# Norms between the blocks of a transformer stack, taken by halves of the tokens

## What is computed

```python
def rms_norm(x, g):
    y = x * lax.rsqrt(jnp.mean(x * x, axis=-1, keepdims=True) + NORM_EPS)
    return y * g

h = rms_norm(x, pre)                      # norm before the block
m = mixer(h)                              # or silu(h @ w_gate) * (h @ w_up) @ w_down
x = x + rms_norm(m, post)                 # norm behind the block, added to the stream
```

## Time and profile before

| what | us |
|---|---|
| median of three runs | 1984.16 (1982.49 to 1985.83) |
| the profiled execution | 1984.12 |
| its span, first to last instruction | 1982.3 |
| PE busy | 1939.0 (98% of the span) |
| DVE busy | 837.3 (42%) |
| ACT busy | 415.3 (21%) |
| POOL busy | 1199.4 (61%) |

### The profile page before, as it was taken

One profiled execution on the slowest core, in us unless ns is written; L12 is line 12 of the kernel. 1 busy time (PEld: TensorE's weight loads), 2 busy tenths in 40 slices (PEclk: granted clock), 3 DMA queues, 4 the chain that ended last, 5 costly groups with the idle time before them and its releaser, 6 DMA issues.

```text
span 1982.3 us, 24733 instructions
## 1 busy us (share of the span) xinstructions
PE 1939.0 (98%) x8948; PEld 1530.6 (77%) x8948; DVE 837.3 (42%) x1341; ACT 415.3 (21%) x820; POOL 1199.4 (61%) x678
## 2 busy tenths in 40 slices
PE   8999989999999999999999999999999999999998
PEld 6876557888888877877778888887878778888886
DVE  7345872543431035345254334113894463434102
ACT  3444751211110021015131111001234331111000
POOL 6973445766666646650576666665767566666652
PEclk9999999999999999999999999999999999999999
DMA  5441002233233212320223333321323223223311
GB/s 199 129 118 42 1 1 85 65 97 94 95 119 102 76 54 86 96 85 1 81 69 95 95 95 109 104 84 54 96 75 106 75 64 106 87 94 114 102 59 43
DMA packets 43818, 166.13 MB, mean 84 GB/s; under 512 B 5088, under 2 KB 5344, under 8 KB 43744
## 3 DMA queue, kind: packets, MB, share of 16 engines
q1 hardware_dynamic: 42912, 162.99, 25.9%
q10 hardware_dynamic: 832, 2.11, 0.3%
HBM read 162.97 MB, written 2.10 MB: 83 GB/s over the span
## 4 chain that ended last, share of the span: by engine, by line
PE 87%; DVE 4%; ACT 1%; issue 1%; POOL 0%; POOLq 0%; DVEq 0%; ACTq 0%
PE psum L489 26%; PE psum L491 26%; PE psum L490 26%; PE psum L521 1%; PE psum L654 1%; PE psum L668 1%; PE psum L730 1%; PE psum L542 1%; PE psum L748 1%; DVE e_ring L1382 1%; PE psum L550 1%; PE psum L695 0%; PE psum L682 0%; PE psum L739 0%; POOL x L421 0%
## 5 line engine op out<-in xcount | busy, mean ns | idle before, releaser
L413 POOL TENSOR_TENSOR w_lo<-raw,w_hi 128x1024 fp32r<-128x1024 f32 (+1 forms) x287 | 752.9, 2623 | 23.9
L489 PE MATMUL psum<-h_hi,w_hi 128*128 128x512 f32 x1704 | 679.2, 399 | 11.6 <-DVE h_lo L1298 4.1
L410 POOL TENSOR_SCALAR w_hi<-raw 128x1024 fp32r<-128x1024 f32 (+1 forms) x287 | 325.0, 1132 | 601.2 <-PE psum L491 567.5
L490 PE MATMUL psum<-h_lo,w_hi 128*128 128x512 f32 x1704 | 675.4, 396 | 0.0
L491 PE MATMUL psum<-h_hi,w_lo 128*128 128x512 f32 x1704 | 675.3, 396 | 0.0
L489 PEld LDWEIGHTS psum<-h_hi,w_hi 128*128 128x128 f32 x1704 | 321.4, 189 | 93.5 <-issue 7.0
L491 PEld LDWEIGHTS psum<-h_hi,w_lo 128*128 128x128 f32 x1704 | 321.3, 189 | 78.0
L490 PEld LDWEIGHTS psum<-h_lo,w_hi 128*128 128x128 f32 x1704 | 321.5, 189 | 76.9 <-issue 0.7
L489 PE MATMUL psum<-g_hi,w_hi 128*128 128x512 f32 x528 | 208.8, 396 | 0.0
L490 PE MATMUL psum<-g_lo,w_hi 128*128 128x512 f32 x528 | 208.8, 396 | 0.0
L491 PE MATMUL psum<-g_hi,w_lo 128*128 128x512 f32 x528 | 208.8, 396 | 0.0
(11 more groups left out here) (261 smaller groups left out, 1779.0 us busy)
## 6 DMA issues: line engine op xcount, KB each, us to landing
raw<-in_wide SPq DMA_DIRECT2D x239, 512.0 KB, 3.5
raw<-in_down SPq DMA_DIRECT2D x48, 704.0 KB, 4.0
x<-in_xt ACTq DMA_DIRECT2D x4, 512.0 KB, 7.3
out<-x SPq DMA_DIRECT2D x8, 256.0 KB, 2.0
o_diff<-in_angles SPq DMA_DIRECT2D x1, 512.0 KB, 7.2
cols<-in_cols SPq DMA_DIRECT2D x1, 221.0 KB, 4.6
tabs<-in_tables SPq DMA_DIRECT2D x1, 208.0 KB, 6.0
k_fox<-forget ACTq DMA_DIRECT2D x8, 2.0 KB, 1.9
```

Of the source, the lines that this page charges most:

```text
L410: nc.gpsimd.tensor_scalar(w_hi[:, slot, 0:w], raw[:, j % RAW, 0:w], 1.0, 1.0, ALU.mult, ALU.mult)\
L413: nc.gpsimd.tensor_tensor(w_lo[:, slot, 0:w], raw[:, j % RAW, 0:w], w_hi[:, slot, 0:w].bitcast(F32), ALU.subtract).then_inc(units_split, 1)
L489: pe.matmul(out_ap, lhs[0], rhs[0], start=first, stop=False)
L490: pe.matmul(out_ap, lhs[0], rhs[1], start=False, stop=False)
```

## The change

The unit of the norm becomes a half chunk: 256 tokens of one feature chunk, H = 256. Half chunk k is chunk k % 8 of tokens 0 to 255 for k below 8, and of tokens 256 to 511 above.

- **Last unit.** `last_unit` multiplies the last unit of the block for tokens 0 to 255 first, into one bank, then for tokens 256 to 511 into another. Between the two stand the sums over the partitions for the first half; the row for the first half is spread behind the third tile of the second. In the down projection the first 11 tiles of the last chunk are split in two as well. `post_stat` with its matmuls of ones is gone.
- **Opening.** `opening_by_halves` takes TOGETHER = 3 units in step, 9 matmuls of 256 columns for each of 16 half chunks. The sums for tokens 256 to 511 stand behind half chunk 0, their row (now in bank 7) behind half chunk 2. A fourth unit follows alone in matmuls of 512 columns, with `col_stat` behind its first tile and `row_stat` behind its fourth.
- **DVE, ACT, POOL.** Scaling, adding, `h_hi` and `h_lo` are done by half chunks; `tmp` is used as four buffers of 256. DVE still does the first add, POOL the other 15. `add_norm` stands behind the split of the third unit, so the fourth unit's split is behind the last add. Squares of x for the new norm keep their 512 columns.
- **The end.** DVE does six of the sixteen last adds, POOL ten; sixteen DMAs of 128 KB take x out.
- The one-turn loop around the last four chunks of the down projection is written out.

The diff, cut to its core (`half_variance`, `half_inverse`, `last_out` and ACT's `last_square` are the old steps on a slice of the tokens):

```diff
+TOGETHER = 3
+H = S // 2
...
+FINAL_BY_DVE = (0, 3, 6, 9, 12, 15)
...
+def of_half(k):
+    return slice((k // KC) * H, (k // KC + 1) * H)
...
+            for k in range(2 * KC):
+                if k in FINAL_BY_DVE:
+                    sp.wait_ge(x_final, FINAL_BY_DVE.index(k) + 1)
+                else:
+                    sp.wait_ge(x_ready, 5 * 2 * KC + sum(j not in FINAL_BY_DVE for j in range(k + 1)))
+                sp.dma_start(out[:, k % KC, of_half(k)], x[:, k % KC, of_half(k)]).then_inc(stored, 16)
+            sp.wait_ge(stored, 16 * 2 * KC)
...
-            def add_norm():
-                n.take("post_scaled")
-                for c in range(1, KC):
-                    pool.wait_ge(post_scaled, n.take("post_scaled"))
-                    nc.gpsimd.tensor_tensor(x[:, c, :], x[:, c, :], tmp[:, c % 2, :], ALU.add).then_inc(x_ready, 1)
+            def add_norm(by_dve=(0,)):
+                for k in range(2 * KC):
+                    n.take("post_scaled")
+                    if k in by_dve:
+                        continue
+                    pool.wait_ge(post_scaled, n.now("post_scaled"))
+                    part = x[:, k % KC, of_half(k)]
+                    nc.gpsimd.tensor_tensor(part, part, tmp_half(k), ALU.add).then_inc(x_ready, 1)
...
-                cuts = [(at + SLOTS, add_norm) for at in NORMS_AT[:-1] if u < at + SLOTS <= u + count]
+                cuts = [(at + TOGETHER, add_norm) for at in NORMS_AT[:-1] if u < at + TOGETHER <= u + count]
...
-            def post_stat():
-                stay_warm(1, STAT_ROW)
-                col_stat()
-                stay_warm(1, STAT_ROW, blocks=2)
-                row_stat()
-                stay_warm(4, STAT_COL)
...
+            def last_squares(blocks):
+                pe.wait_ge(squared, n.take("squared"))
+                add_columns(squares[:, (KC - 1) % 2, :], False, blocks[-1] == NB - 1, blocks)
+            def last_unit(h, tiles, banks, first):
+                w = next_unit()
+                for t in range(tiles):
+                    mm = three(psum[:, banks[0], 0:H], [w[0](t), w[1](t)], [part[:, 0:H] for part in h(t)], first and t == 0, t == tiles - 1)
+                mm.then_inc(half_done, 1)
+                pe.wait_ge(summed, n.take("summed", SUMS))
+                n.take("squared", KC - 1)
+                add_columns(total, True, False)
+                last_squares((0, 1))
+                for t in range(tiles):
+                    mm = three(psum[:, banks[1], H:S], [w[0](t), w[1](t)], [part[:, H:S] for part in h(t)], first and t == 0, t == tiles - 1)
+                    if t == 2:
+                        row_stat((0, 1))
+                mm.then_inc(unit_done, 1)
...
+            def opening_by_halves():
+                banks, units = [], []
+                for u in range(TOGETHER):
+                    banks.append(next_bank())
+                    units.append(next_unit())
+                start = n.base["h_low"]
+                n.take("h_low", 2 * KC)
+                for k in range(2 * KC):
+                    t = k % KC
+                    pe.wait_ge(h_low, start + k + 1)
+                    for u in range(TOGETHER):
+                        mm = three(psum[:, banks[u], of_half(k)], [units[u][0](t), units[u][1](t)], [h_hi[:, t, of_half(k)], h_lo[:, t, of_half(k)]],
+                                   t == 0, t == KC - 1)
+                        if k == 2 * KC - 1:
+                            mm.then_inc(unit_done, 1)
+                    if k == 0:
+                        last_squares((2, 3))
+                    if k == 2:
+                        row_stat((2, 3), STAT_COL)
+                bank, unit = next_bank(), next_unit()
+                for t in range(KC):
+                    mm = three(psum[:, bank, :], [unit[0](t), unit[1](t)], h_of(t), t == 0, t == KC - 1)
+                    if t == 0:
+                        col_stat()
+                    if t == 3:
                         row_stat()
+                mm.then_inc(unit_done, 1)
...
+                for u in range(KC - OPEN - 1):
                     feature_unit(h_of, bank=next_bank())
-                post_stat()
+                banks = [next_bank(), next_bank()]
+                last_unit(h_of, UNIT, banks, True)
...
+                banks = [next_bank(), next_bank()]
+                w = next_unit()
+                for t in range(DOWN_UNIT):
+                    for j in range(2):
+                        mm = three(psum[:, banks[j], j * H:(j + 1) * H], [w[0](t), w[1](t)], [part[:, j * H:(j + 1) * H] for part in hidden_of(0)(t)],
+                                   t == 0, False)
+                mm.then_inc(unit_done, 1)
+                last_unit(hidden_of(1), DOWN_UNIT, banks, False)
...
+            def norm(pre, k, bias=None):
+                def high(j):
+                    act.wait_ge(x_ready, n.take("x_ready"))
+                    copy(h_hi[:, j % KC, of_half(j)], x[:, j % KC, of_half(j)], scale=col(pre, j % KC)).then_inc(h_high, 1)
+                high(0)
+                last_square(k, 1, bias)
+                high(1)
+                high(2)
+                roots(slice(2, NB))
+                for j in range(3, KC):
+                    high(j)
+                for c in range(KC + 1):
+                    if c < KC:
+                        high(KC + c)
+                    if c:
+                        square(c - 1, x[:, c - 1, :])
...
+                def scale(k):
+                    if k >= 4:
+                        added(k - 4)
+                    if k % KC == KC - 1:
+                        dve.wait_ge(evacuated, final_base + k // KC + 1)
+                    row = psum[:, STAT_COL if k >= KC else STAT_ROW, of_half(k)]
+                    v.scalar_tensor_tensor(tmp_half(k), m[:, k % KC, of_half(k)], col(post, k % KC), row, ALU.mult, ALU.mult).then_inc(post_scaled, 1)
+                def add(k):
+                    dve.wait_ge(post_scaled, scaled_base + k + 1)
+                    part = x[:, k % KC, of_half(k)]
+                    v.tensor_tensor(part, part, tmp_half(k), ALU.add).then_inc(x_ready if pre else x_final, 1)
...
+                half_variance(2, slice(0, 2))
+                last_out(m, 0, bias)
+                half_inverse(slice(0, 2))
+                dve.wait_ge(row_spread, n.take("row_spread"))
+                scale(0)
+                add(0)
+                scale(1)
+                low(0)
+                scale(2)
+                n.take("unit_done", units)
+                last_out(m, 1, bias)
                 if pre:
+                    scale(3)
+                    low(1)
+                    half_variance(1, slice(2, NB))
+                    low(2)
+                    scale(4)
+                    half_inverse(slice(2, NB))
+                    low(3)
+                    scale(5)
+                    scale(6)
+                    low(4)
+                    scale(7)
+                    low(5)
+                    dve.wait_ge(row_spread, n.take("row_spread"))
+                    for k in range(8, 2 * KC + 2):
+                        if k < 2 * KC:
+                            scale(k)
+                        low(k - 2)
+                        if k >= KC + 3:
+                            add_square(k - KC - 3)
                     n.take("squared")
+                else:
+                    half_variance(1, slice(2, NB))
+                    scale(3)
+                    half_inverse(slice(2, NB))
+                    add(3)
+                    for k in range(4, 2 * KC):
+                        if k == KC:
+                            dve.wait_ge(row_spread, n.take("row_spread"))
+                        scale(k)
+                        if k in FINAL_BY_DVE:
+                            add(k)
+                n.take("x_ready", 2 * KC)
+                n.take("post_scaled", 2 * KC)
```

162 lines of the change are left out of this document (79 added, 83 removed).

## The result

| | before | after |
|---|---|---|
| median, us | 1983.60 (1982.49 to 1985.83, 4 runs) | **1961.95** (1961.32 to 1962.44, 4 runs) |
| profiled execution; its span | 1984.12; 1982.3 | 1961.61; 1959.8 |
| PE busy | 1939.0 | 1908.8 |

The ratio is 0.9889, 95% interval 0.9872 to 0.9906: the changed kernel is 1.1% faster. The forecast was 1964 us.

What follows compares the result with a forecast made beforehand. PE was taken as the bound, losing 8.77 us without products at each of five boundaries. Savings of 4.1 + 2.6 + 3.4 + 3.9 + 3.4 and 3.1 at the end, 20.5 us, gave 1964 us; range 1957 to 1977.

Steps and rivals of the forecast that it cites:

- The last unit and the first wait: Last unit behind `w_out`: halves 5.76, sums, spreads and returns 1.84, PE's wait for the first half of `h_lo` 0.8 us.
- The half-width matmul: Each 256-column matmul on PE was put at 0.12 us, with 0.117 and 0.13 as ends of the range.
- The opening: Three units by half chunks: matmuls 17.28, sums, spreads and returns 0.99, then a 0.9 us wait.
- The wait ahead of the fourth unit: PE waits 0.9 us for POOL's `w_lo` at five boundaries, the price of moving `add_norm` ahead of that split.
- The fourth unit: Whole unit behind the opening: 24 full-width matmuls, sums, spreads and two returns, 8.28 us.
- The chain at boundary 2: The next block hangs on `scale_row` there: 2.6 us saved, PE's 3.9 us wait growing some 1.3.
- fewer POOL splits: Fox layer's chain meets fewer POOL splits; with 0.117 a matmul, part of more than forecast, 1954 to 1959, chance 0.09.
- The end: Program end: x finished 20.7 us behind the last unit's start, 3.1 us saved.
- The clock: Forecast: clock holds at boundaries. Rival: it falls in every one, giving about 1973 us, chance 0.05.
- Halves that do not halve: Rival: 256-column matmuls take 0.18 us, a 48 us loss, 2032; beyond 1988, chance 0.07.
- Ports in full: Rival: DVE and POOL never overlap in the opening, 1.25 us a half chunk; 1982 us, chance 0.06.
- The next block hanging on `scale_row` everywhere: Rival: each boundary saves only 2.3 to 2.6, sum 16, 1968 us; counted within 1959 to 1969, chance 0.56.

Runs made afterwards that it cites:

- stat_behind: Changed kernel with the last unit's column sums, first-half squares and spread moved behind both halves, opening by halves kept; ratio to the kernel before 1.0007.
- units_halved: Kernel before with only its ordinary eight-tile 512-column units computed as two 256-column halves; ratio to the kernel before 1.0012.
- squares_later runs: Changed kernel with the forget gate's unit fourth and DVE's adds of squares one or two steps later; ratios to the kernel before 0.9850 and 0.9820.
- after_again: The changed kernel run again unaltered, beside the variants with later adds of squares; ratio to the kernel before 0.9881.
- two_together: Changed kernel with two units in step by halves instead of three, and two whole units behind them; ratio to the kernel before 1.0042.
- forget_fourth: Changed kernel with the forget gate's unit moved from first to fourth place in the fox layer's projection; ratio to the kernel before 0.9856.
- last_add_dve: Changed kernel with the sixteenth half-chunk add of each inner norm on DVE instead of POOL; ratio to the kernel before 0.9932.
- squares_later_2: forget_fourth with DVE's adds of squares two steps later and ACT's squares one step later; 1949.0 us, ratio to the kernel before 0.9820.
- final_by_pool: Changed kernel with 15 of the last norm's 16 adds on POOL instead of ten; ratio to the kernel before 0.9889.
- squares_later_1: forget_fourth with DVE's adds of squares one step later in the opening; ratio to the kernel before 0.9850.

## Why the prediction was right, point by point

- **The last unit and the first wait.** Forecast 5.76 + 1.84 + 0.8 = 8.4 us from the last unit's start to the opening's first product; measured 8.33 (330.86 to 339.19). Two errors cancel in it: matmuls and sums took 7.29 and not 7.60, and the stop behind them is 1.04 and not 0.8 (0.88 of it wait, in the row). The forecast's own terms, 2.4 against 1.88 and 0.14 of pick-up, give 0.66 and not 0.8; the chain took 2.84, from the end of the spread (336.35) to the first product. The cover by the second half is the mechanism: without it the gain is gone (stat_behind), though some 1.8 of the 4.3 us lost there are clock.
- **The half-width matmul.** Forecast 0.12; 24 take 2.73 us in the last unit, 0.114, and the thousands of units_halved say 0.117. The low end of the range was right. It is worth 0.3 us in a last unit (5.46 for 5.76) and, with waits between, 0.4 in an opening; boundaries 3 and 5 beat the forecast by 0.6 each.
- **The opening.** Forecast 17.28 + 0.99 + 0.9 = 19.2, measured 18.8. The wait ahead of the fourth unit, forecast 0.9, stands five times with 0.75 to 1.02. My cause was POOL's order; the squares_later runs show that DVE's adds of squares, which hold POOL's last adds back, are what makes it late. The sum had these adds in it, but I read the result as the price of moving `add_norm`. The time of POOL's last add came out, 15.9 us behind the start of the first low part (338.15 to 354.01) for a forecast of 16.0, but the parts did not: low parts beside an add take 0.57 in place of 0.47, in six rows, where I had eleven of them 0.21 late, and waits of DVE for PE and ACT (0.31 and 0.39) that I had not laid in make up for part of it. Nor is the pace even, as the forecast's 0.99 a half chunk has it: it is 0.88, and 1.38 once the adds of squares start.
- **The fourth unit.** Forecast 8.28, measured 8.27 (998.71 to 1006.98) at boundary 3.
- **The chain at boundary 2.** Forecast: saved 2.6 and a wait grown to some 5.2. Measured: a wait of 6.12, and from this last unit's start to the next one's 265.7 us instead of 266.8, so 1.1 saved. This is the term with the largest error. `scale_row` starts 36.1 us behind the last unit's start, not 34.9, since the fourth unit ran partly at the lower clock (34.3 in after_again, which had no such stretch there and saved 3.2). The chain from there to PE's next matmul grew from 13.6 to 14.5. I had given "fewer POOL splits" a chance. The chain does meet one fewer (the last step, the scan, takes 1.21 for 1.94), but it meets another near its start and is held 1.44 us longer.
- **The end.** x final 20.4 us behind the last unit's start (forecast 20.7), the program's end 2.3 us later, saved 3.6 (forecast 3.1).
- **The clock.** The forecast let it hold everywhere. In after it drops once more than I allowed, at boundary 2; the boundaries 1 and 4 of before lost 0.7 us each to it that is now back, of which I had booked only the first: at the fourth I took 3.9 where PE's own saving stood at 4.6, because `scale_row` might be late there, and it was not (no wait of PE stands behind it).
- **The rivals.** Halves that do not halve: excluded by 9120 matmuls. Ports in full: no, 1982 was not reached, and half chunks came every 0.88 us beside each other's work in two_together, not every 1.25. The next block hanging on `scale_row` everywhere: only at boundary 2. The clock: at one boundary of five, 1.5 us, not at all of them.

So the sum of 20.5, against some 22 measured, came out for largely the right reasons: the cover, the half-width price and the wait for `w_lo` are where they were said to be. That it is so near is partly luck. At boundary 2 the forecast was 1.5 us too high, at the other five places 0.5 to 1.3 too low, and the 1.6 us lost in the conformer and the 1.7 gained ahead of boundary 1, neither of which was forecast, nearly cancel.

## What to carry to other kernels

Where a reduction over a whole unit stands between two dense stretches, split it by columns, so that half of the unit covers the other half's statistics; count the half-width matmuls as half, and then look at the vector side, because the covering engine has to be slower than it by a little and no more. Before an engine is given part of another's work, look at what runs on the sharing partner at that instant: an add of 0.42 us that started just behind an instruction of 2.4 cost 2.2 of waiting. A chain of small dependent steps belongs where its engine has caught up with the producer, not first in the block.

## What the runs showed of the hardware

- **DVE and POOL.** A DVE operation that reads only SBUF and is issued during a POOL instruction ended 0.27 to 0.55 us behind it in these traces, whatever its own length: 2.58 us for an add of 0.42, 2.72 for an 8-partition step that took 1.28 before. I had laid this to two SBUF inputs. The gate's `TENSOR_SCALAR` with one input (8 x 512, the rows below, POOL then DVE) is held too: 1.79 us beside a split that ends at 744.93. In forget_fourth a TENSOR_SCALAR of the same shape, with no split beside it, takes 0.41. The Trainium skill (SBUF — State Buffer, SBUF: two separate sides) has both: the pair of ports is also taken by a DVE operation in a 2-port mode, and whichever starts first keeps it for the whole instruction. These rows agree that a one-input operation is held, and add the 0.27 to 0.55 us; in which mode it ran no row shows. It works the other way too: POOL's `w_hi` of the fourth unit, issued 0.05 us behind a low part, takes 1.34 instead of 1.04 us. Operations with one PSUM input are not held: scalings and adds of squares keep 0.47 and 0.68 beside POOL. Between POOL's `w_hi` and `w_lo` there is 0.1 us, and a low part that waits there gets its turn first (last_add_dve, 358.40; squares_later_2, 353.39).

```profile
742.54 2.39 POOL L426 TENSOR_TENSOR w_lo<-raw,w_hi 128x1024 fp32r<-128x1024 f32 x1
...
743.42 1.79 DVE L1799 TENSOR_SCALAR forget<-forget,cols 8x512 f32<-8x512 f32 x1
```

In forget_fourth, DVE:

```profile
758.65 0.41 DVE L1805 TENSOR_SCALAR forget<-forget 8x512 f32<-8x512 f32 x1
```

- **The clock behind small waits.** In several profiles some of the units behind the opening ran nine full matmuls in 3.7 us instead of 2.2, at the lower level, just behind the wait for `w_lo` and the column sums: one boundary of five in after, after_again and final_by_pool (not always the same one), two in forget_fourth and squares_later_1, all five in two_together, where the wait is 1.34 us, and none in squares_later_2, where it is 0.21 us or less. In the changed kernel it was this window (735 to 745 us: length, busy PE, PEld, DVE, ACT and POOL, clock):

```profile
735.00:745.00 10.00, 10.00 (x50) 8.55 (x49) 3.29 (x5) 1.49 (x2) 9.73 (x7) 0.83 0.52 157
```

  A stretch costs 1.4 to 1.5 us. That the shorter wait prevents it fits most of these profiles; it is not shown, since squares_later_1 had two with waits of 0.32, and four boundaries of after had none with waits of 0.76 to 1.02.
- **Scatter ahead of the first boundary.** In kernels that are alike up to there its last unit starts between 330.2 and 336.3 us, so spans of single executions compare only from that point on.
